# Eight attention units of a streaming encoder layer: loops over the units on every engine, and the same units written out in a row

## What is computed

```python
z  = rms_norm(x, g_attn) @ w_in             # q, k, v of 8 + 4 heads, forget column, two gates
oA = softmax(qa @ ka.T / 8 + decay, causal) @ va       # 8 heads of 64, decay = cumsum(log f)
oB = (softmax(s1) - lam * softmax(s2)) @ vb            # 4 heads, two 64-wide maps, 128-wide values
x1 = x + (sigmoid(gate_a) * (oA @ w_oa) + sigmoid(gate_b) * (rms_norm(oB) @ w_ob)) @ w_out
y  = x1 + (silu(a) * b) @ w_down                       # [a|b] = conv3(rms_norm(x1) @ w_up)
```

## Time and profile before

| | us |
|---|---|
| median of three runs | 1921.44 |
| lowest and highest | 1918.46 and 1921.92 |
| the profiled execution's own time | 1918.76 |
| its span, first to last instruction | 1916.9 |
| PE busy | 1782.4 (93% of the span) |
| DVE busy | 1134.8 (59%) |
| ACT busy | 780.5 (41%) |
| POOL busy | 109.7 (6%) |
| first scores of units 1, 2, 3, 4 and 5 on PE | at 217.89, 329.61, 435.96, 540.68 and 639.72 |

### The profile page before, as it was taken

How to read it: one execution, slowest core, us unless ns; L and a number is a source line. 1 busy time by engine, 2 the same in 40 slices (tenths; PEclk the granted TensorE clock), 3 DMA queues, 4 the chain that set the end, 5 groups by cost and what they waited for, 6 DMA issues and landing times.

```text
span 1916.9 us, 32874 instructions
## 1 busy us (share of the span) xinstructions
PE 1782.4 (93%) x12029; PEld 1313.2 (69%) x12029; DVE 1134.8 (59%) x2345; ACT 780.5 (41%) x1328; POOL 109.7 (6%) x184
## 2 busy tenths in 40 slices
PE   5989997999999999996999989999999999999997
PEld 3556665666656565554999976668976679766797
DVE  6465655656476767666654478774247762477621
ACT  5546554555556565555321234442013331133311
POOL 3110101000010101000000000000000000000011
PEclk9989998999999999998999999999999999999999
DMA  6250607043322313133433211111111111111121
GB/s 187 91 154 19 187 0 205 1 100 107 77 85 63 98 45 114 28 100 117 130 123 111 80 34 45 54 44 56 44 34 54 44 47 42 45 44 55 41 86 47
DMA packets 152997, 145.45 MB, mean 76 GB/s; under 512 B 7928, under 2 KB 133986, under 8 KB 152912
## 3 DMA queue, kind: packets, MB, share of 16 engines
q1 hardware_dynamic: 134176, 78.29, 15.2%
q0 software_dynamic: 18736, 65.98, 10.6%
HBM read 113.14 MB, written 31.11 MB: 75 GB/s over the span
## 4 chain that ended last, share of the span: by engine, by line
PE 78%; DVE 8%; issue 5%; ACT 5%; DMA 3%; POOL 0%; DVEq 0%; ACTq 0%; SPq 0%; POOLq 0%
PE bank L758 43%; PE psS L758 17%; PE psO L758 11%; PE psT L974 2%; DMA gate<-gate_scr 2%; DMA cum_s<-c_scr 1%; DVE sc L1876 1%; PE psT L758 1%; DVE peak_w L1618 1%; ACT pT_h L1160 1%; PE bank L786 1%; ACT sc L1392 1%; DMA x_tm<-in_x_prompt 1%; DVE m_a L1974 0%; DVE m_b L1974 0%
## 5 line engine op out<-in xcount | busy, mean ns | idle before, releaser
L758 PE MATMUL bank<-xn_hi,w_h 128*128 128x364 f16 (+1 forms) x984 | 316.2, 321 | 8.7 <-ACT v_tm L1160 2.6
L758 PE MATMUL bank<-xn_lo,w_h 128*128 128x364 f16 (+1 forms) x984 | 315.7, 321 | 0.0
L758 PE MATMUL bank<-xn_hi,w_l 128*128 128x364 f16 (+1 forms) x984 | 314.9, 320 | 0.0
L758 PE MATMUL psS<-x_h,wf_l 128*128 128x364 f16 (+1 forms) x528 | 167.7, 318 | 0.0
L758 PE MATMUL psS<-x_h,wf_h 128*128 128x364 f16 (+1 forms) x528 | 167.7, 318 | 0.0
L758 PE MATMUL psS<-x_l,wf_h 128*128 128x364 f16 (+1 forms) x528 | 167.7, 318 | 0.0
L1523 ACT ACTIVATE ct<-u,vecs 128x1090 f32<-128x1090 f32 x44 | 57.1, 1297 | 259.0 <-DVE u L2091 233.4
L758 PEld LDWEIGHTS bank<-xn_hi,w_h 128*128 128x128 f16 x984 | 97.1, 99 | 73.1 <-issue 10.5
L758 PEld LDWEIGHTS bank<-xn_hi,w_l 128*128 128x128 f16 x984 | 97.3, 99 | 56.9 <-issue 1.7
L758 PEld LDWEIGHTS bank<-xn_lo,w_h 128*128 128x128 f16 x984 | 97.2, 99 | 49.5 <-issue 1.1
L1605 DVE SCALAR_TENSOR_TENSOR pT_l<-psT,pT_h 128x1024 f16<-128x1024 f32 (+8 forms) x72 | 54.4, 756 | 122.5 <-ACT pT_h L1160 122.5
(11 more groups left out here) (367 smaller groups left out, 4221.2 us busy)
## 6 DMA issues: line engine op xcount, KB each, us to landing
wraw<-in_w_up SPq DMA_DIRECT2D x44, 512.0 KB, 3.9
wraw<-in_w_in SPq DMA_DIRECT2D x41, 512.0 KB, 7.8
gate<-gate_scr POOLq DMA_DIRECT2D x16, 544.0 KB, 4.4
wraw<-in_w_down SPq DMA_DIRECT2D x16, 448.0 KB, 3.7
cum_s<-c_scr POOLq DMA_DIRECT2D x8, 544.0 KB, 7.9
x_scr<-xT POOLq DMA_DIRECT2D x8, 544.0 KB, 7.3
sqq<-rt_scr SPq DMA_DIRECT2D x16, 272.0 KB, 4.3
sqk<-rt_scr SPq DMA_DIRECT2D x16, 272.0 KB, 5.6
```

The lines of the kernel that those rows point to most:

```text
L758: return pe.matmul(out, w, x, start=first, stop=last, **kw)
```

## The change

In `units`, and in the stream of SP, the loops are gone: the same `body` is emitted for u = 0 to 7 (on SP 0 to 6) with u a constant. Plans, tiles, buffers, matmuls and DMAs are the same; no item moves against another.

```diff
@@ -488,12 +488,8 @@
 
     def units(e, body):
 
-        with e.Fori(0, 3) as u:
-            body(Unit(u, "A", True))
-        body(Unit(3, "A", True))
-        with e.Fori(4, 7) as u:
-            body(Unit(u, "B", True))
-        body(Unit(7, "B", False))
+        for u in range(UNITS):
+            body(Unit(u, "A" if u < 4 else "B", u < 7))
 
@@ -566,13 +562,8 @@
-        with sp.Fori(0, 2) as u:
-            body(Unit(u, "A", True))
-        for u in (2, 3):
-            body(Unit(u, "A", True))
-        with sp.Fori(4, 6) as u:
-            body(Unit(u, "B", True))
-        body(Unit(6, "B", True))
+        for u in range(UNITS - 1):
+            body(Unit(u, "A" if u < 4 else "B", True))
```

## The result

The changed kernel takes 1902.93 us, median of 7 runs (1901.67 to 1909.19), against 1919.06 for the kernel before, 7 runs beside it. The ratio is 0.9924, 95% interval 0.9915 to 0.9933: 14.6 us less, 12.9 to 16.3 (the two medians are 16.1 apart). The forecast was 1905.6, from 1900 to 1911, faster with 0.92.

The account below looks back on a forecast made before the run. PE, busy 93% of the span, was taken as the bound, so only its idle or lower-clock time could be won. Terms 8.8 + 4.8 + 0.9 = 14.5 us, from a base of 1920.1, gave 1905.6 us, range 1900 to 1911.

Parts of the forecast that it names:

- Term 1, the slow branch: PE's jump back ahead of unit 2: the 7.21 us stall and the clock's 2.09 us go; 8.8 us won.
- in straight code there is no jump, so both parts go: At unit 2's start, the 7.21 us between units and 2.09 us from the lower clock vanish, 9.30 in all.
- Term 2, the table load: ACT's tanh table load at job G00 starts before the bank wait: 1.33 us in units 0-2, 0.27 in 4-6; 4.8 us.
- Term 3, POOL: At unit 3's start, POOL issues the last `cum_s` load earlier without register work between its DMAs; 0.9 us won.
- 5 us or more before each unit's start: Sign expected in the changed trace: POOL issues the last `cum_s` load that far ahead of each unit.
- Terms at nothing, register work: Register instructions ahead of waits on all engines: at most 0.3 us in unit 1, left out of the sum.
- units 4 to 6 shorter by more than 1 us each: Sign that the prediction was wrong; these units were forecast at 98.6 to 98.9 us.
- Loading straight code costs nothing: Fetching all of PE's written-out code costs 0 as long as loading stays ahead of PE.
- the third, stalls elsewhere: Rival: slow branches or unloaded blocks elsewhere on PE, 7.3 us each plus clock; chance 0.04 for three or more, 0.04 for two.
- The first, only the idle time goes: Rival: at unit 2's start the clock falls anyway, or table loads are delayed; win 7 to 10.6 us, chance 0.10.
- The second, more than the sum: Rival: table loads worth 1.33 us each in units 4-6, `cum_s` loads earlier; win 17 to 21 us, chance 0.12.
- The last, that the change does nothing beyond terms 2 and 3: Rival: the slow branch is one execution's accident, not in the median; 5.7 us, 1914 to 1915 us, chance 0.03.

Follow-up runs that it names:

- the one jump alone: Kernel before with PE's first loop over units 0 and 1 only and unit 2 written out; 1909.61 us, ratio 0.9946.
- the run with the moved code: Kernel before with 110 semaphore increments ahead of PE's first work, moving its first loop's body; 1925.99 us, ratio 1.0031.
- the moved load: Changed kernel with POOL issuing the next unit's `cum_s` load ahead of its last store; run twice, 1902.90 and 1900.65 us.
- the run with the two terms alone: Kernel before with PE written out and, in ACT's loops, job G00's wait for the filled bank behind the table load; 1907.83 us, ratio 0.9942.
- the waits swapped: Kernel before, all loops kept, with ACT's wait for the filled bank behind the table load for job G00; 1912.21 us, ratio 0.9956.

## Why the prediction was right

The time, the direction and the two large terms were as forecast; both small terms were mis-sized. That the sum came out to 0.1 us is luck: the small errors cancel, and the interval of the win is 3.4 us wide.

*Term 1, the slow branch: 8.8 us, bounds 7.0 to 9.3.* Right in cause and size. PE's code written out alone gave 8.1, the one jump alone 10.4, and one slow jump more cost 6.0. The stretch from the end of unit 1 to the start of unit 3 fell by 9.4 us where terms 1 and 2 made 10.1 of it. The clock was 1.00 through the starts of units 1 to 3. The reading of the earlier trace rows, code loaded again, is borne out by the packets of the run with the moved code; why the code was missing is open (below). The step "in straight code there is no jump, so both parts go" was true, and PE written out was sufficient but not needed: with ACT written out and PE looped the stall was gone too.

*Term 2, the table load: 4.8 us, bounds 3.6 to 8.0.* Right. It was priced by the earlier trace rows at 1.33 for each of three units and by the earlier trace rows at 0.27 for each of three; the runs gave 1.2, 1.14 and 1.29, and 0.26, 0.26 and 0.22, in all 4.3. PE's own idle rows of 1.19 and 0.27 were the better price of the two, as taken for units 4 to 6.

*Term 3, POOL: 0.9 us, bounds 0 to 1.8.* Mis-sized: it measured 0.15 us. The step that failed is "written out, POOL has no register work between its DMAs, so I give back the 0.9 of the issue". The load for unit 3 is issued 4.44 us ahead of the start in the changed kernel and 4.43 with POOL alone written out, against 4.28 before, where the term gave back 0.9. So most of unit 3's later issue is not POOL's register work. The sign "5 us or more before each unit's start" came in unit 1 alone (5.09, 4.97, 4.44). What the term rested on, that PE pays for this load's landing, was right, and the moved load shows it: 1.3 to 2.0 us in each of units 1 to 3 against the changed kernel's first trace, 0.8 to 1.9 against its second.

*Terms at nothing, register work.* Mis-sized too, the other way. The step was read in units 1 and 3, which are alike, and carried to units 4 to 6, which are not. In unit 4 PE idles 1.17 us less, of which the table load is 0.26. The other 0.9 us comes from ACT, DVE and POOL written out, shown engine by engine; whether it is the register instructions or waits that stand elsewhere in straight code, as the one ahead of job G00 does, no run tells apart. In units 0 to 2 it is nothing, as I had it: the changed kernel's first trace idles 4.86, 4.75 and 5.37 us there, and the run with the two terms alone 4.60, 4.64 and 5.22. I had written that units 4 to 6 shorter by more than 1 us each would be wrong; units 4 and 5 were (1.25 and 1.1), unit 6 was not (0.5). Units 5 and 6 are each 0.8 us shorter in the mean of the two traces of the changed kernel, of which 0.25 is the table load; the rest is not register work as far as the traces show, since the run with the two terms alone has them as short (196.39 us together, against 196.38 and 196.28). The two errors, 0.7 too much in term 3 and 0.9 too little in unit 4, cancel by luck.

*Loading straight code costs nothing*: right, but the evidence was weaker than I took it for. 72 packets came in place of 59, and no stall. I had units 4 and 5 take the same time to 0.01 us; in those rows PE idles 8.07 us in unit 4 at a clock of 1.00 and 6.81 in unit 5 at 0.98, so the equal lengths were chance. *The rivals*: the third, stalls elsewhere, did not come; L1094, PE's loop of the earlier trace rows, stayed at or below 209 ns. The first, only the idle time goes, is refuted by the clock of 1.00 at unit 2's start. The second, more than the sum, 17 to 21 us, is outside the interval of 12.9 to 16.3. The last, that the change does nothing beyond terms 2 and 3, would have been 5.7 us and lies below it.

*The base.* The median of before over 7 runs beside the changed kernel is 1919.06; I had taken 1920.1 between the execution and three runs. The win was forecast as 14.5 and came as 14.6; the 2.7 us by which the time was too high are the base and the scatter of either median.

What stays open is why, in the kernel before, only the second of two like jumps is slow. The run with the moved code shows that the address of the body matters. The seven kernels that keep PE's loop over units 0 to 2 show that something outside PE matters too: with ACT in its loops the second jump is slow in all five traces, with ACT written out it is quick in both. Neither DVE nor POOL written out does that. With the waits swapped ACT's table load comes as early as in straight code (in unit 1 it begins 0.02 us behind `root`), and the trace still has the slow jump, so that shift alone does not remove it in every execution. No run changed ACT's program without changing its timing, so which of the two it is wasn't told apart.

## What to carry to other kernels

The jump back of PE's long loop cost 0.2 us or 6 to 7.5 here, and the branch's own rows, minimum, median and maximum, tell which; look at the maximum, since one slow jump in three hides in a median. Where a loop and a written-out pass of the same body stand in one trace, compare them in PE's idle time beside the length: in the five traces with ACT, DVE and POOL written out, unit 4's idle time repeated to 0.05 us where its length spread over 1.9. And carry a price from one kind of unit to another only with a row of that other kind: writing ACT, DVE and POOL out was worth nothing beyond the table load in the first kind and 0.9 us in the second.

## What was not expected of the hardware

PE's jump back took 7.3 us or 0.21 with the same PE program, by whether ACT's was written out. Adding 110 instructions ahead of the loop made the first jump slow too.

A late DMA cost twice here, once as PE's idle time and once more by the clock that fell behind it. The second run with the moved load has unit 2 at a mean granted clock of 0.97, 4.9 us longer than units 1 and 3, of which 2.5 us are PE's busy time and 2.4 its idle time. The idle time came first. The chain (start, length, what), PE's timeline, and the windows around the wait and the fall:

```profile
398.81 10.19 DMA sqk<-rt_scr
...
412.34 0.45 PE L824 MATMUL bank<-ident,kc_tm 128*128 128x128 f32 x1 [2.52 <-ACT sqq L1235]
...
319.79:409.82 90.03, 87.87 (x717) 58.68 (x716) 49.54 (x141) 49.72 (x97) 6.48 (x10) 1.00 0.23 62
409.82:412.34 2.52, 0.00 (x1) 0.03 (x1) 2.52 (x4) 0.56 (x1) 0.00 (x0) 0.98 1.05 363
412.34:419.00 6.66, 5.84 (x25) 4.16 (x26) 4.68 (x10) 4.14 (x8) 1.41 (x2) 0.50 1.16 294
```

The last load of `sqk` for the unit took 10.19 us, where the median of these loads on that trace's page is 5.6. DVE and ACT waited for it and PE for them, 2.52 us, and then the clock stood at its lower level for the next 6.7 us. In the first run with the moved load the same place has 0.22 us of idle time in units 1 and 2 and no fall of the clock in units 1 to 3. The moved `cum_s` loads are on their way at that time in both, so they may be what made `sqk` late; that isn't shown. ACT alone written out had the same order of events in unit 3 (108.00 us), with `cum_s` as the late load.

One such event is as large as term 2, so the lengths of one profiled execution against another say little about 3 us; the windows say in which unit it fell.
